# Attention results kept by channel: regrouped column halves, sums divided in the output projection

## The reference

```python
# block one, per layer (grouped-query heads and neighbourhood heads)
p = jax.nn.softmax(s, axis=-1);  o = einsum('bgrqs,bsgd->bqgrd', p, vals)
y_l = concat([yr_l * silu(rg_l), ya_l * silu(ag_l), yn_l * silu(ng_l)]) @ w_out
x = _layer_norm(DEEPNORM_ALPHA * x + gate[:, None] * y_l, ln_g, ln_b)
# block two, per layer (forget, stick-breaking, latent and memory heads, four each)
probs = softmax(where(mask, logits, -inf));  o = einsum('bhqk,bhkd->bhqd', probs, v)
mixed = concat([out_fox, out_sb, out_mla, out_mem])
y = einsum('bsc,cd->bsd', mixed * silu(gate), w_out[l])
h_res = _layer_norm_2(DEEPNORM_ALPHA_2 * h_res + y, ln_g[l], ln_b[l])
```

## Time and profile before

| | |
|---|---|
| median of 3 runs | 4729.49 us (4725.6 to 4730.8) |
| profiled execution, span | 4720.0 us |
| TensorE busy, share of the span | 4091.5 us, 87% |
| VectorE / ScalarE / GpSimd busy | 2738.4 / 1553.0 / 1499.3 us |
| four attention stages, fills at the front cut off | 1064 us, TensorE busy 998.06 |
| four output projections, steady part | 291 us, TensorE busy 290.80 |
| mean granted clock of TensorE | 0.938 of full speed |

### The profile page before, as it was taken

The page is one execution under the profiler, slowest core; times in us unless marked ns, Lnnn a source line. Parts: engine busy times, 40 slices in busy tenths (PEclk is TensorE's granted clock), DMA queues, the critical chain, the costliest instruction groups (busy, mean ns, idle before and its releaser), DMA issues. The chain is left out here.

```text
span 4720.0 us, 105768 instructions
## 1 busy us (share of the span) xinstructions
PE 4091.5 (87%) x43986; PEld 3144.1 (67%) x43986; DVE 2738.4 (58%) x4666; ACT 1553.0 (33%) x2721; POOL 1499.3 (32%) x1210
## 2 busy tenths in 40 slices
PE   6999788869999699878886999599679889968898
PEld 4878688835657587668874667488436667853566
DVE  3465455556657457545556666755657656557565
ACT  1333233325542133223324552200355420025542
POOL 2233144411004323324422013654132145514214
PEclk8999899979999899999998999699899999989899
DMA  5445523261235546633333224433312443340325
GB/s 195 155 172 194 164 74 86 70 220 33 63 82 180 161 145 211 204 110 90 83 112 91 61 65 167 154 110 102 121 35 68 129 159 101 106 141 7 83 58 182
DMA packets 555145, 560.12 MB, mean 119 GB/s; under 512 B 196092, under 2 KB 449564, under 8 KB 552660
## 3 DMA queue, kind: packets, MB, share of 16 engines
q1 hardware_dynamic: 427156, 475.95, 32.5%
q10 hardware_dynamic: 127616, 78.95, 5.8%
HBM read 366.75 MB, written 192.23 MB: 118 GB/s over the span
## 5 line engine op out<-in xcount | busy, mean ns | idle before, releaser
L1096 PE MATMUL pr_acc<-hH,pr_wh 128*128 128x512 f32 (+1 forms) x1288 | 481.2, 374 | 0.0
L1097 PE MATMUL pr_acc<-hL,pr_wh 128*128 128x512 f32 (+1 forms) x1288 | 465.5, 361 | 0.0
L1098 PE MATMUL pr_acc<-hH,pr_wl 128*128 128x512 f32 (+1 forms) x1288 | 465.2, 361 | 0.0
L2634 ACT ACTIVATE an_p<-an_p,an_stat 128x1280 f32<-128x1280 f32 (+5 forms) x372 | 340.5, 916 | 163.2 <-DVE an_stat L2712 157.7
L2574 PE MATMUL an_t<-ident,an_p 128*128 128x128 f32 x2152 | 320.4, 283 | 40.9 <-ACT an_pT L2641 27.9
L2574 PEld LDWEIGHTS an_t<-ident,an_p 128*128 128x128 f32 x2152 | 237.1, 142 | 164.8 <-issue 67.1
L2667 POOL TENSOR_TENSOR an_kl<-an_k,an_kh 128x1280 fp32r<-128x1280 f32 (+3 forms) x36 | 78.5, 2182 | 841.7 <-DVE an_qh L2692 841.7
L2708 DVE CUSTOM_DVE_ANT_0 an_p<-an_s,an_mask 128x256 f32<-128x256 f32 (+8 forms) x308 | 274.8, 892 | 100.6 <-PE an_s L2557 67.8
L1465 POOL TENSOR_TENSOR sp_sl<-sp_w,sp_sh 128x512 fp32r<-128x512 f32 x172 | 246.0, 1437 | 197.4 <-DVE sp_sh L1540 179.0
L2599 PE MATMUL an_oacc<-an_pT,an_v 128*64 128x512 f32 (+3 forms) x1224 | 298.8, 562 | 4.0 <-DVE an_pT L2719 1.9
L2004 DVE TENSOR_TENSOR rk_tu<-rk_tu,rk_ps 128x512 f32<-128x512 f32 x300 | 188.8, 682 | 190.5 <-PE rk_ps L1828 190.5
(11 more groups left out here) (383 smaller groups left out, 9942.0 us busy)
## 6 DMA issues: line engine op xcount, KB each, us to landing
CHK<-ri_out SPq DMA_DIRECT2D x24, 1920.0 KB, 8.0
rk_in<-CHK SPq DMA_DIRECT2D x240, 128.0 KB, 2.4
pr_w<-in_w_in ACTq DMA_DIRECT2D x58, 512.0 KB, 4.3
UT<-pr_out SPq DMA_DIRECT2D x45, 640.0 KB, 4.7
sp_w<-in_w_in ACTq DMA_DIRECT2D x50, 512.0 KB, 5.2
U<-sp_c SPq DMA_DIRECT2D x100, 256.0 KB, 2.0
mod_w<-in_w_mod SPq DMA_DIRECT2D x16, 1024.0 KB, 8.3
mo_w<-in_w_out SPq DMA_DIRECT2D x16, 1024.0 KB, 9.8
```

The costliest lines, as they stand in the source:

```text
L1096: nc.tensor.matmul(out, wh[:, u, k, 0:m], hi, start=(k == 0), stop=False)
L1097: nc.tensor.matmul(out, wh[:, u, k, 0:m], lo, start=False, stop=False)
L1098: ins = nc.tensor.matmul(out, wl[:, u, k, 0:m], hi, start=False, stop=(k == KT - 1))
L2634: nc.scalar.activation(row, row, ACT.Exp, bias=stat[:, n % NPM, j, 1:2], scale=heads[groups[n][0]].scale, accum_out=total[:, n % 4, j:j + ...
```

## The change

**Attention.** The two column halves now take neighbouring query blocks: half 0 the blocks 0 and 1 of a group, half 1 the blocks 2 and 3. Each key block is multiplied once for each half, over 256 columns at most, and both accumulate over all key blocks. Nothing is left to add, so *final*, *norm* and the constant `pair` are gone. *out* is now the reciprocal and a copy of 128x256; `an_oT` and `an_rcp` have four buffers. *store* is one DMA per half, 64 channels by up to 256 tokens, to the new scratch tensor `YCM` (channels as rows), and one of the reciprocals, single 4-byte elements, to `RCP` (heads as rows). *exp* of group n waits for *out* of n-4.

**Output projection.** The block's result is loaded from `YCM` with channels on partitions, in runs of 512 B. Two (block one) or four (block two) further DMAs bring the reciprocals from `RCP`, each head's row repeated over its 64 partitions. A new GpSimd step, `divided`, multiplies both (128x640 or 128x1024) before VectorE gates the result. The turns (218) are gone, and the PSUM of the stage goes from 8 banks to 4. GpSimd first sets the whole table to one, for channels that have no sum, and SP's first load waits for that.

**Stick-breaking.** The turns of the result (32) and ScalarE's copies of them (8) are gone; `sb_oT` is stored to `YCM` as it is.

```diff
-    RANK = {"final": 0, "out": 0, "norm": 0, "vturn": 1, ...
+    RANK = {"out": 0, "vturn": 1, ...
...
 # weigh (TensorE)
-                        for half in range(2):
-                            k = 2 * p + half
-                            cs = columns(n, k)
-                            ins = nc.tensor.matmul(O[half * HD:(half + 1) * HD, cs], V[:, c % 2, blocks[n][k], :],
-                                                   PT[:, buffer(n, k), cs], start=(p == 0), stop=(p == len(blocks[n]) // 2 - 1),
-                                                   skip_group_check=True)
+                        for k in (2 * p, 2 * p + 1):
+                            for a in range(2):
+                                part = part_of(n, k, a)
+                                if part is None:
+                                    continue
+                                to = O[a * HD:(a + 1) * HD, 0:2 * P].rearrange("d (j t) -> d j t", t=P)[:, part, :]
+                                ins = nc.tensor.matmul(to, V[:, c % 2, blocks[n][k], :], by_query(PT[:, buffer(n, k), :], a)[:, part, :],
+                                                       start=(k == 0), stop=(k == len(blocks[n]) - 1), skip_group_check=True)
                         ins.then_inc(pv.sem, 1)
-                    if kind == "final":
-                        bank = free_bank(kind, x)
-                        pe.wait_ge(oo.sem, oo.nth(x + 1))
-                        for j in range(len(spec[x])):
...
 # store (SP)
+                        sp.wait_ge(oo.sem, oo.nth(x + 1))
+                        for a in range((k + 1) // 2):
+                            to = core.t["YCM"][row:row + HD, first:first + k * P].rearrange("d (j t) -> d j t", t=P)
...
+                            sp.dma_start(core.t["RCP"][row // HD, first:first + k * P].rearrange("(j p) -> p j", p=P), rcp[:, u, 0:k]) \
...
 # output projection
-                    sp.dma_start(yt_in[:, u, :], T["YTOK"][tok:tok + P, 0:nt * P]).then_inc(y_in.on(u), 16)
+                    sp.dma_start(yt_in[:, u], T["YCM"][0:nt * P, tok:tok + P].rearrange("(k p) t -> p k t", p=P)).then_inc(y_in.on(u), 16)
+                    for j0, j1 in summed_tiles:
+                        for a in range(2):
+                            row = T["RCP"][2 * j0 + a:2 * j1:2, tok:tok + P].unsqueeze(0).to_broadcast([HD, j1 - j0, P])
+                            sp.dma_start(rb[a * HD:(a + 1) * HD, u, j0:j1, :], row).then_inc(y_in.on(u), 16)
...
+                def divided(t):
+                    u = t % 2
+                    pool.wait_ge(y_in.on(u), y_in.step(t, u))
+                    nc.gpsimd.tensor_tensor(yt_in[:, u], yt_in[:, u], rb[:, u], ALU.mult).then_inc(yn.sem, 1)
...
                 for t in range(nblk):
+                    if t + 2 < nblk:
+                        divided(t + 2)
                     power(t)
                     if t + 2 < nblk:
                         lower(t + 2)
...
-                turn(0)
                 first_product()
                 for t in range(1, nblk):
-                    if t + 1 < nblk:
-                        turn(t + 1)
                     product(t)
...
-                    dve.wait_ge(tr.sem, tr.nth(t + 1))
...
+                    dve.wait_ge(yn.sem, yn.nth(t + 1))
+                    V.scalar_tensor_tensor(YT[:, u, ncm:NK, :], gt[:, u], 0.5, yt_in[:, u], ALU.mult, ALU.mult).then_inc(yt.sem, 1)
```

More of the change, by code:

```diff
@@ L2224, in rwkv_output @@
           + [(mm, 2 * N)])
[L2227 removed]
+Head = namedtuple("Head", "q kv nq d scale groups bias row")
 KeyValue = namedtuple("KeyValue", "k v nk")
+QUERY_HALVES = ((0, 1), (2, 3))
+NOUT = 4
 class Order:
[L2236 removed]
+    RANK = {"out": 0, "vturn": 1, "vcopy": 1, "weigh": 2, "copy": 2, "prep": 2, "aug": 2, "score": 3, "max": 3, "turn": 4, "exp": 4}
     def __init__(self, heads, kvs):
@@ L2321, in parts @@
                 need += [("vcopy", v) for v in self.values(c)] + ([("out", n - 1)] if n else [])
-            work["weigh", x] = ({"PE": 0.1 + 0.22 * len(self.members(n, 2 * p))}, need, 0.1)
+            widest = [max(len(self.half_members(n, k, a)) for a in range(2)) for k in (2 * p, 2 * p + 1)]
+            work["weigh", x] = ({"PE": 0.1 + 0.22 * sum(widest)}, need, 0.1)
         for n in range(len(self.groups)):
[L2324 to L2327, removed]
+            work["out", n] = ({"DVE": 0.6}, [("weigh", (n, len(self.blocks[n]) // 2 - 1))] + ([("store", n - NOUT)] if n >= NOUT else []), 0.1)
+            work["store", n] = ({"SP": 1.6}, [("out", n)], 3.0)
         return work
@@ L2345, in place @@
                 engines, need, _ = work[key]
-                if kind in ("turn", "vturn", "final") and len(uses) >= 2:
+                if kind in ("turn", "vturn") and len(uses) >= 2:
                     held = uses[-2]
-                    need = need + [({"turn": "copy", "vturn": "vcopy", "final": "norm"}[held[0]], held[1])]
+                    need = need + [({"turn": "copy", "vturn": "vcopy"}[held[0]], held[1])]
                 if any(k not in ended for k in need):
@@ L2740, in attention @@
-    counts = [(zeroed, 16 + 3), (hi, len(heads)), (lo, len(heads)), (lk, sum(opens)), (au, aug_no[-1]), (vt, vturns_to(len(kvs) - 1)), (qk, NS), (mxs, NS), (mx, NS),
-              (ex, NS), (tg, len(o.turns)), (pv, len(o.weighs)), (fz, NG), (oo, NG), (rec, NG), (neg, int(any_bias)), (given_back["ACT"], o.given["ACT"]),
+                        if n >= NOUT:
+                            dve.wait_ge(stored[u].sem, stored[u].after(0) + stored_to(n - NOUT))
+                        V_.reciprocal(rcp[:, u, 0:k], total[:, n % 4, 0:k])
@@ L3221, in _ @@
                 weigh(NS - 1)
-                for x in turning[NS]:
-                    turn(*x)
             @block.scalar
```

169 lines of the change are left out of this document (68 added, 101 removed).

## The result

The changed kernel takes 4917.56 us (median of 4 runs, 4913.78 to 4924.47) against 4730.15 us for the kernel before on the same chip: ratio 1.0398, 95% interval 1.0383 to 1.0413. It is 187 us slower where 110 us less were forecast. The profiled execution has a span of 4922.6 us, 202.6 more than in the earlier trace rows.

A forecast was written before the change was run, and what follows sets the result against it. TensorE's own instruction list was taken to bound attention (94% busy) and the output projection. Terms -84 - 6 + 6 - 4 - 5 - 17 = -110 us gave 4620 us, 8-in-10 range 4580 to 4685.

The forecast's parts named there:

- the reciprocals' store: Attention: storing reciprocals as single four-byte elements costs under 1 us per group, only the last group's showing.
- SP's loads: Attention: SP issues about 190 more transfers; next head's loads, issued several groups ahead of use, are not delayed: cost nothing.
- Rival 4: Attention: SP, with three transfers a group, hands loads out late; little or no gain, near 4725 us; chance 0.04.
- Rival 3: Attention: column halves take turns on TensorE instead of overlapping, +230 us of streaming; about 4845 us; chance 0.05.
- rivals 1 and 2: Rival 1: finals half hidden, 4677 us, chance 0.22; rival 2: finals, bank waits, turns in full, 4587 us, chance 0.13.
- The finals: Attention: all 98 last turns of the query blocks leave TensorE, 88% realised: -84 us (-48 to -100).
- the banks: Attention: 98 uses of a bank for turned probabilities are freed, so turns wait less: -6 us (0 to -16).
- the weighing: Attention: regrouped matmuls, 1124 for 612, with no overhead per matmul counted: +6 us (-2 to +8).
- the tails: Ends of the four attention stages: VectorE's normalisation goes, more issues and a longer landing come: -4 us (0 to -6).
- The stick-breaking stages: Result stored straight from the copy: 1.4 us at each of two ends, 2 us for six other turns: -5 (-2 to -8).
- The projection: Output projection: turns go -24 us, late operands from GpSimd's multiply +4, later starts +3: -17 us (-24 to +16).
- the steady part: Output projection mid-stage: TensorE never waits, so its turns go in full, -24 us, less +4 where GpSimd's multiply delays operands.

The follow-up runs named there:

- the turned table: The changed kernel with all reciprocals of a stage kept in one SBUF table, turned once on TensorE and stored as rows of 512 B: 4648.55 us, 0.9843.

## Why the prediction was wrong

**The step that failed** is the cost of the reciprocals' store: "the price is under 1 us per group and only the last group's shows", and with it SP's loads at "cost nothing". I priced it by the nearest row, a vector loaded element by element. That is a read from memory into SBUF. A store puts neighbouring four-byte elements into memory, and that row could not show what this does. It held the loads behind it by 9 us, and 34 us went at the four ends, 11 us each in place of 2.4. Adding these stores to the old kernel costs 186 us; writing the same bytes as rows in the new one gains 282. The cover was misjudged too: loads were said to be issued "several groups ahead of use". In the third attention stage of the kernel before, VectorE took up the keys of a latent head 9.0 to 14.2 us after the first load's issue, one to one and a half times the 9.1 us that a group takes, and 2.6 to 3.7 us after the last packet; a hold-up of 9 us could not be hidden.

The Trainium skill (DMA: Bandwidth & Descriptors, Specifications) says that under 512 B the engine reads, modifies and writes. I had weighed that as a few us at the ends. By size alone the rule doesn't foretell the runs either: four-byte pieces 64 B apart cost nothing that the time shows. The traces show where the time goes, in 4 KB packets of the loads behind, up to 10.6 us each, and not in the packets of the elements; 406 such packets take 2 us or more in the changed kernel, none with rows or with the turned table, one with the elements 64 B apart. What makes them wait stays open. A read and write-back of a stretch that several pieces share would fit, but no trace shows it, nor the size of such a stretch.

**Rival 4** had the place, loads that come late, but not the cause (SP's issues) nor the price, and a chance of 0.04. Rival 3 did not happen; rivals 1 and 2 spoke of gains within a mechanism that another hid.

**What was right.** The finals, the banks, the weighing and the tails were put at -88 us; with the stores of elements out of the way the four stages fall from 1146.8 to 1056.0, -91, and the gaps behind them grow by 0.7 each. The total agrees; the four terms were not measured apart. No overhead per matmul shows in the weighing. The stick-breaking stages gave 16 us, not 5; two ends of 1.4 account for 3, so the rest must lie in the turns inside them, which I had taken for mostly hidden.

**What was wrong beside it.** The projection, forecast at -17, has +47 us from the end of attention to its own end: +34 lie between the stages, +12 at the starts, and the steady part gave 0 in place of -20. The starts are explained only in part: with the turned table, they come 6 us earlier in all without SP's wait for the table set to one and with the gates ahead. For the steady part, "In the steady part TensorE never waits, so they go in full" was the error: an engine that is 99.9% busy bounds a short stretch, but in block one a loop of other engines at 11.6 us stood behind TensorE's 11.45 already, held by GpSimd's shift, and in block two the multiply, put on GpSimd, stretched VectorE's gate from 1.2 to 3.05 us.

The sum of what was measured: +157 attention, +47 projection with the ends, -16 stick-breaking, 188 of the 202.6 us; the other 15 are spread over stages that the change leaves alone. TensorE's mean granted clock in the third attention stage fell to 0.81 (0.95 in the run with rows), and its busy time rose to 202 us from the 176 of that run; I have not parted this from the waits. In the prediction's sum the lower ends of the terms add up to -156, not -154; nothing hangs on it.

## What to carry to other kernels

Price a small store by a row that writes to memory in the same layout, not by a read of the same size; where neighbouring pieces of a few bytes come from many partitions, turn them on chip and store rows, or put them apart. A transfer that nobody waits for can still cost its neighbours: look at GB/s against DMA share behind it. And before counting the whole of what is taken from a full engine, look at the step from one instruction to its next round on every other engine: where that is already as long as the full engine's, or where a wait for it shrinks from block to block, a second loop is there.

## What was not expected of the hardware

512 stored elements of 4 B side by side hold up the transfers behind them for some 9 us, also those of another queue: single 4 KB packets of the loads then take up to 10.6 us, while the elements' own take 7 to 9 ns. As 128 runs of 16 B they cost about 1 us, and 64 B apart nothing that the time shows (4728.84 against 4725.74 us). And in block one a VectorE sum of 128x1024 with both operands in SBUF, 1.22 us by itself, ended 1.08 us after the GpSimd operation that it ran beside, whenever it had started, so that it took up to 2.40; the sum that reads PSUM took 1.21 beside the same operation.
